# Norm factors as exp(-ln/2) on ScalarE in place of square root and reciprocal, with the last squares summed by TensorE and smaller last stores

## What is computed

```python
def rmsnorm(x, g):
    xf = x * lax.rsqrt(jnp.mean(x * x, axis=-1, keepdims=True) + 1e-6)
    return xf * g
def swiglu_ffn(x, g, w_in, w_out):
    h = rmsnorm(x, g) @ w_in
    gate, up = jnp.split(h, 2, axis=-1)
    return (jax.nn.silu(gate) * up) @ w_out
# the layer
x = x + 0.5 * swiglu_ffn(x, norm_ffn1, w_ffn1_in, w_ffn1_out)
parts = rmsnorm(x, norm_mix) @ w_in            # ssd head group and attention head group
y = concatenate([rmsnorm(ssd(parts), g1), rmsnorm(nsa(parts), g2)])
x = x + y @ w_out
x = x + mem_attend(rmsnorm(x, norm_mem_q), mem_kv(rmsnorm(mem, norm_mem_kv)))
x = x + 0.5 * swiglu_ffn(x, norm_ffn2, w_ffn2_in, w_ffn2_out)
y = rmsnorm(x, norm_final)
```

## Time and profile before

| | us |
|---|---|
| median of 3 runs | 2840.41 (2838.55 to 2842.89) |
| the profiled execution, whole time | 2840.38 |
| its span in the trace | 2838.7 |
| TensorE busy | 2697.9 (95%) |
| VectorE busy | 1418.0 (50%) |
| ScalarE busy | 717.4 (25%) |
| GpSimd busy | 344.1 (12%) |
| mean granted TensorE clock | 0.973 of full speed |

### The profile page before, as it was taken

How to read it: one execution, slowest core, us unless ns; L and a number is a source line. 1 busy time by engine, 2 the same in 40 slices (tenths; PEclk the granted TensorE clock), 3 DMA queues, 4 the chain that set the end, 5 groups by cost and what they waited for, 6 DMA issues and landing times. The chain is left out here.

```text
span 2838.7 us, 43914 instructions
## 1 busy us (share of the span) xinstructions
PE 2697.9 (95%) x17720; PEld 2529.8 (89%) x17720; DVE 1418.0 (50%) x2949; ACT 717.4 (25%) x1466; POOL 344.1 (12%) x294
## 2 busy tenths in 40 slices
PE   8999999999989998989789988899999999999996
PEld 7999999999989997879557765797899999999996
DVE  7444444444466222335567753676644444444445
ACT  5111111111042212212456652435411111111102
POOL 0000000000020000101157761220100000000003
PEclk9999999999999999989889998899999999999998
DMA  6111111111025325114120004102211111111101
GB/s 215 45 45 45 46 45 45 45 45 45 16 96 67 53 76 192 59 38 116 42 61 16 2 22 177 60 23 90 75 45 45 45 45 45 45 45 45 41 5 63
DMA packets 62989, 168.42 MB, mean 59 GB/s; under 512 B 10468, under 2 KB 43780, under 8 KB 52996
## 3 DMA queue, kind: packets, MB, share of 16 engines
q1 hardware_dynamic: 57716, 150.36, 16.8%
q10 hardware_dynamic: 3104, 9.41, 0.9%
q0 software_dynamic: 1968, 5.77, 0.6%
HBM read 145.90 MB, written 23.69 MB: 60 GB/s over the span
## 5 line engine op out<-in xcount | busy, mean ns | idle before, releaser
L523 DVE TENSOR_TENSOR ffn_gated<-ffn_gate_up,ffn_inv_rms 128x728 f32<-128x728 f32 x132 | 120.6, 914 | 536.9 <-PE ffn_gate_up L206 536.7
L204 PE MATMUL ffn_gate_up<-h_ffn_hi,ffn_up_hi 128*128 128x364 f32 (+1 forms) x1056 | 349.1, 331 | 15.1 <-DVE h_ffn_lo L102 11.5
L204 PE MATMUL ffn_down<-ffn_act_hi,ffn_down_hi 128*128 128x364 f32 (+1 forms) x1056 | 349.9, 331 | 7.8 <-issue 6.2
L204 PE MATMUL ffn_gate_up<-h_hi,ffn_up_hi 128*128 128x364 f32 (+1 forms) x1056 | 347.5, 329 | 2.6 <-DVE ffn_gated L523 1.0
L205 PE MATMUL ffn_gate_up<-h_ffn_lo,ffn_up_hi 128*128 128x364 f32 (+1 forms) x1056 | 347.8, 329 | 0.0
L205 PE MATMUL ffn_down<-ffn_act_lo,ffn_down_hi 128*128 128x364 f32 (+1 forms) x1056 | 347.8, 329 | 0.0
L206 PE MATMUL ffn_gate_up<-h_ffn_hi,ffn_up_lo 128*128 128x364 f32 (+1 forms) x1056 | 347.7, 329 | 0.0
L206 PE MATMUL ffn_down<-ffn_act_hi,ffn_down_lo 128*128 128x364 f32 (+1 forms) x1056 | 347.3, 329 | 0.0
L205 PE MATMUL ffn_gate_up<-h_lo,ffn_up_hi 128*128 128x364 f32 (+1 forms) x1056 | 346.9, 329 | 0.0
L206 PE MATMUL ffn_gate_up<-h_hi,ffn_up_lo 128*128 128x364 f32 (+1 forms) x1056 | 346.9, 328 | 0.0
L557 DVE SCALAR_TENSOR_TENSOR x<-ffn_down,x 128x364 f32<-128x364 f32 (+1 forms) x480 | 248.0, 533 | 148.0 <-PE ffn_down L206 148.0
(11 more groups left out here) (469 smaller groups left out, 4739.5 us busy)
## 6 DMA issues: line engine op xcount, KB each, us to landing
ffn_up_raw<-in_w_ffn_in SPq DMA_DIRECT2D x42, 1024.0 KB, 4.8
ffn_down_raw<-in_w_ffn_out SPq DMA_DIRECT2D x22, 1024.0 KB, 4.8
mix_w_raw<-in_w_mix SPq DMA_DIRECT2D x20, 512.0 KB, 3.4
scratch_x<-x SPq DMA_DIRECT2D x1, 4352.0 KB, 12.8
out_proj<-mix_stage ACTq DMA_DIRECT2D x8, 544.0 KB, 2.7
x<-scratch_x SPq DMA_DIRECT2D x1, 4352.0 KB, 16.9
cmp_w<-in_cmp_w SPq DMA_DIRECT2D x2, 2048.0 KB, 14.6
ssd_pages<-in_cmp_pages SPq DMA_DIRECT2D x32, 128.0 KB, 2.0
```

What stands on the lines that cost most here:

```text
L204: pe.matmul(out, w_hi, x_hi, start=start, stop=False)
L523: dve.tensor_tensor(zu[:, b, :, 0:w], gu[:, b, :, 0:w], inv[:, groups(g)].rearrange("p (o c) -> p o c", o=1).to_broadcast([P, 2, w]), ALU. ...
```

## The change

1. root and invert become one function, factor, on ScalarE: Ln of the mean square plus eps, then Exp with scale -0.5, in place. The semaphore from the root to DVE becomes one from Ln to Exp on ACT itself, and DVE waits for the Exp. All 22 reciprocals of norms go (3 in each of the ffn, mix and final norms, 9 in the out stage, 1 for the memory keys). In the out stage factor's Exp carries the waits that invert had.
2. A Ln of one column is added at the start of each ffn close and at the end of the sample attention, so that the table is loaded there.
3. In the final norm, factors 0 and 1 come behind square 11 and 19 in place of 12 and 20. The last tile's squares are no longer added by POOL: TensorE adds them with a second matmul into the same bank.
4. The last group's stores are four of 2 tiles, in place of two of 4.

```diff
-    def root(self, act, g):
+    def factor(self, act, g):
+        at = self.inv[:, groups(g)]
         if self.late is not None and g:
             act.wait_ge(self.late_summed, g)
-        act.activation(self.inv[:, groups(g)], self.sums[:, g, 0:width_of(g)], ACT.Sqrt, bias=self.core.eps[:, 0:1]
-                       ).then_inc(self.rms_ready, 1)
-    def invert(self, dve, g):
-        dve.wait_ge(self.rms_ready, g + 1)
-        dve.reciprocal(self.inv[:, groups(g)], self.inv[:, groups(g)]).then_inc(self.inv_ready, 1)
+        act.activation(at, self.sums[:, g, 0:width_of(g)], ACT.Ln, bias=self.core.eps[:, 0:1]).then_inc(self.log_ready, 1)
+        act.wait_ge(self.log_ready, g + 1)
+        act.activation(at, at, ACT.Exp, scale=-0.5).then_inc(self.inv_ready, 1)
...
+        mm = pe.matmul(out, self.ones[:], self.acc[g][:, 0:width_of(g)], start=True, stop=stop and direct is None)
+        if direct is not None:
+            pe.wait_ge(self.sq_ready, direct + 1)
+            mm = pe.matmul(out, self.ones[:], self.sq[direct % len(self.sq)][:, 0:width_of(g)], start=False, stop=stop)
+        mm.then_inc(self.summed, 1)
...
         for g in range(GROUPS):
+            size = KT // 2 if g < GROUPS - 1 else 2
+            for k in range(0, KT, size):
+                sp.wait_ge(self.y_ready, g * KT + k + size)
...
                 def close():
+                    act.activation(log_table[:], core.eps[:, 0:1], ACT.Ln)
...
-                        if fin is not None and d in (KT + lag, 2 * KT + lag):
-                            fin.roots(act, d // KT - 1)
+                        if fin is not None and d in (KT + lag - 1, 2 * KT + lag - 1):
+                            fin.factor(act, d // KT - 1)
...
                     rounds(2)
-                    root(1)
-                    root(2)
+                    factor(1)
+                    factor(2)
                     split_up(1, 1, False)
...
                 def factor(g):
-                    parts.invert(dve, g)
                     dve.wait_ge(parts.inv_ready, g + 1)
+                    if g == 2:
+                        dve.wait_ge(act_ready, 1)
                     scale(0, 0, g)
...
-                def root(i):
+                def factor(i):
...
+                    act.activation(logs[:, i % 2, 0:c], ms[:, i % 2, 0:c], ACT.Ln, bias=core.eps[:, 0:1]
+                                   ).then_inc(log_ready, 1)
+                    act.wait_ge(log_ready, i + 1)
+                    if i >= 3:
+                        old = UNITS[i - 3]
+                        act.wait_ge(h_ready[old[0:2]], KT if old[0] == "x" else 4 * (old[2] + 1))
+                    act.activation(inv[:, i % 3, 0:c], logs[:, i % 2, 0:c], ACT.Exp, scale=-0.5).then_inc(inv_ready, 1)
```

More of the change, by code:

```diff
@@ L156, in add, with sum @@
         pool.tensor_tensor(acc, acc, sq, ALU.add).then_inc(self.added, 1)
-    def sum(self, pe, g, last, stop=True):
+    def sum(self, pe, g, last, stop=True, direct=None):
+        out = self.bank(g)[:, :width_of(g)]
         pe.wait_ge(self.added, last + 1)
-        pe.matmul(self.bank(g)[:, :width_of(g)], self.ones[:], self.acc[g][:, 0:width_of(g)], start=True, stop=stop
-                  ).then_inc(self.summed, 1)
-class FinalNorm:
[L168 to L174, removed]
-        act.wait_ge(self.running.summed, g + 1)
[L176 to L186, removed]
@@ L397, in _ @@
                     rounds(1)
-                    root(0)
+                    factor(0)
                     head_squares(1)
@@ L1574, in _ @@
                 rounds(1)
-                parts.root(act, 0)
+                parts.factor(act, 0)
                 rounds(2)
-                parts.root(act, 1)
-                parts.root(act, 2)
+                parts.factor(act, 1)
+                parts.factor(act, 2)
                 split(2)
@@ L2721, in _ @@
                 act.wait_ge(ms_ready, 1)
-                act.activation(inv[:], ms[:, 0:W], ACT.Sqrt, bias=core.eps[:, 0:1]).then_inc(rms_ready, 1)
+                act.activation(inv[:], ms[:, 0:W], ACT.Ln, bias=core.eps[:, 0:1]).then_inc(log_ready, 1)
+                act.wait_ge(log_ready, 1)
+                act.activation(inv[:], inv[:], ACT.Exp, scale=-0.5).then_inc(inv_ready, 1)
                 for n in range(2 * MT):
@@ L2978, in _ @@
                     for n in range(KT):
-                        for i in roots_at(g, n):
-                            root(i)
+                        for i in factors_at(g, n):
+                            factor(i)
                         if g == 0 and n + 2 < KT:
@@ L2990, in _ @@
                 query_hi(0, 0)
-                root(index["x", 2])
+                factor(index["x", 2])
                 round_hi("x", 2, 0)
```

83 lines of the change are left out of this document (39 added, 44 removed).

## The result

The changed kernel takes 2849.69 us, median of 20 runs (2838.13 to 2860.22); the kernel before took 2840.43 in 20 runs beside them (2836.33 to 2856.14). The ratio is 1.0030, with a 95% interval from 1.0017 to 1.0042: **8.5 us slower**, between 4.8 and 11.9. The forecast was 2847.6, range 2842.0 to 2852.5.

The account below looks back on a forecast made before the run. TensorE, busy 95% of the span, was taken to bound the kernel, with VectorE alone ending the last close. 0.35 + 6.8 + 5.0 - 4.95 = +7.2 on 2840.38 gave 2847.6 us, range 2842.0 to 2852.5.

Parts of the forecast that it names:

- second ffn head: wait, clock: Head of the second ffn stage: TensorE stands still 4.9 us before product 3, the clock's fall costs 1.9; together +6.8.
- out stage: Out stage: later factors delay weight and normed lo parts, TensorE waits and the clock falls once; +5.0 us.
- first ffn head: Head of the first ffn stage: factor 1 comes later, product 3 starts some 0.8 later; +0.35 us, bounds 0 and 0.8.
- mix, memory keys, tables: Mix stage, memory keys and other stages' table loads: no net cost, 0 us, bounds -1.3 and +0.3.
- last close, VectorE: Last close: factors come sooner, the direct sum saves nothing, VectorE ends 4.05 us sooner.
- stores: Last close: stores of 2 tiles carry half the bytes and land sooner; -0.9 us.
- The loads: Every factor: Ln and Exp stand in different table sets, so loads are real, each costing 1.30 us on ScalarE.
- first rival: Whole kernel: one table set serves Ln and Exp, loads cost next to nothing; about 2824 us, chance 5%.
- P5's wait: Out stage, group 0: w_lo(5) comes late, so TensorE waits 0.8 to 1.0 us at product P5.
- P7 and the squares behind it: Out stage, group 0: the delay runs on to product P7, 0.5 us more, and to group 0's squares, 0.5 more.
- P16's extra: Out stage, group 1: lo parts for product P16 come late, 2.0 to 2.8 us more TensorE idle; 2.0 taken.
- One fall of the clock: Out stage: waits at product P16 and for POOL behind it let the clock fall once, 1.5 us; it may stay out.

Follow-up runs that it names:

- head_order: Changed kernel with the weights of split_up(1, 1) rounded and subtracted earlier at the second ffn head; 2845.62 us, 1.0009 of before.
- out_before: Changed kernel with the out stage's nine factors as square root and reciprocal again; 2846.09 us, 1.0014 of before.
- fixed_two: Changed kernel with split_up(1, 1) rounded ahead of factors 1 and 2 at the second ffn head and the out stage as before; 2836.98 us, 0.9983.
- close_only: Kernel before with only the change's final norm and last close; 2837.36 us, 0.9976 of before.
- close_half_stores: Kernel before with only the last close's change, but the last group stored in two parts of 4 tiles; 2836.43 us, 0.9982.
- no_exp: Changed kernel with a Copy of the same scale in place of Exp in all 22 factors; 2821.23 us, 0.9924 of before.
- close_split: Kernel before with only the last close's change, factor 1 behind square 18, and TensorE taking square 22 directly too; 2836.69 us, 0.9973.

## Why the prediction was right

| term | forecast | measured | by |
|---|---|---|---|
| second ffn head: wait, clock | +4.9, +1.9 | +4.98, 2.2 to 2.8; stage +7.2 | trace; head_order -7.8, out_before +7.2 |
| out stage | +5.0 | +5.3 to +5.7 | out_before |
| first ffn head | +0.35 | product 3 +1.0; first close 0 to 2.4 later | four traces |
| mix, memory keys, tables | 0 | within 1 us at equal clock | fixed_two |
| last close, VectorE | -4.05 | -4.1 (5.3 less 1.2 of clock) | close_only, head_order |
| stores | -0.9 | -1.0 | close_half_stores |
| sum | +7.2 | +8.5 (4.8 to 11.9) | 20 runs |

**The loads.** The forecast hung on them, and no_exp shows it did so rightly: without them the changed kernel is faster than before by 21.6 us, close to the first rival's 2824. One step of the reasoning was wider than its row: the earlier trace rows show that the set in use behind that Exp did not hold Ln, not that no set holds both. It was the list of the built program that settled it.

**The second head** went as reckoned, to 0.1 us in the wait. The clock's part was between the two bounds given.

**The out stage.** The mechanism was right, w_lo(5) and then the lo parts for P16, but that the sum came out is in part luck. P5's wait was put at 0.8 to 1.0 and is 1.14; P7 and the squares behind it were put at 1.0 and cost 0.9 against the trace of before, but only 0.3 against that of close_only, whose stage is the same. P16's extra was put at 2.0 and is 0.9. One fall of the clock was counted, 1.5 us, and two came, at 1848 and at 1887, 9 and 6 matmuls, which cost 1.6 and 1.5. The comparison behind the one fall was wrong as well: at their lower end 1.7 and 1.30 are 3.0 us of idle, not more than 2.60 + 0.66. The start was put at -0.4; P2 starts 1.8 sooner than before, but of that some 1.8 is the low stretch at the stage's start, 21 matmuls before and 8 now (an estimate, 13 times 0.14). From the stage's start to P24 the changed kernel loses 4.6 us against before. The last 1.0 of the stretch's 5.6 arises in the memory attention, where the clock falls behind a wait of 2.2 us in eleven of the twelve traces, kernels with the stage as before among them, and did not in the one of before: no effect of the change.

**The first head is the undersized term.** "Product 3 starts some 0.8 later" held: it waits 2.52 where it waited 1.74, and starts 1.0 later. I let product 4's 0.3 of idle absorb part of that, and that idle is gone. What failed is "+0.35; bounds 0 and 0.8": I had read in the rows that 1.74 costs no clock and that 2.60 does, and did not apply it to this wait of 2.5. Of four traces of kernels with this head, the clock fell behind product 3 in two (the changed kernel, from 42.91, and out_before, at 41.91) and not in two (head_order, fixed_two). Where it fell, 9 to 11 matmuls took 0.14 more, 1.3 to 1.5 us, and the first close started 2.4 and 1.2 later than before; where it did not, 0.0 and 0.8. In the changed kernel:

```profile
42.00 0.40 PE L204 MATMUL ffn_gate_up<-h_ffn_hi,ffn_up_hi 128*128 128x364 f32 x1 [2.52 <-DVE ffn_gated L529]
...
42.73 0.38 PE L205 MATMUL ffn_gate_up<-h_ffn_lo,ffn_up_hi 128*128 128x364 f32 x1
42.91 0.51 PE L206 MATMUL ffn_gate_up<-h_ffn_hi,ffn_up_lo 128*128 128x364 f32 x1
```

**The close.** The steps held one by one: factor 0 earlier, factor 1 bound by ScalarE's four steps, the direct sum worth nothing, y 16 at 38.7 us behind the close's first matmul by the forecast and 37.44 + 1.2 = 38.6 measured at the same clock. What I did not see is that VectorE's two new waits, 1.8 and 2.8, were left for the taking, and that the second is GpSimd's.

**What the sum leaves.** Second head, out, first head and close add up to 7.4 at least and 10.2 at most by the traces, and 8.5 was measured, between 4.8 and 11.9: the medians can't tell the forecast of 7.2 from any of these. Whether the ssd and nsa stages, which took 3.1 us more in the changed kernel's trace, lose anything from the change is not shown; with all kernels between 658.0 and 668.4, the longest in close_split, which holds the change only in its close, and no order by whether they hold the change, I take it as chance. The chances were added up loosely: 0.8 x 51 + 14 + 2 is 57, not 58.

## What to carry to other kernels

Before you replace a function of one table set by two functions, list the loads that the build puts in: here a chain of Ln and Exp cost two loads of 1.28 us nearly each time, whatever one set could hold, and it gains only where nobody waits behind them. When an engine that is mostly idle gets more work, look at what stands behind it in its queue, and move the item that the bound engine needs to the front: one item moved forward in two queues gave back 7.8 us of its stage here, with every load still in place. And a matmul that replaces an add saves nothing when it runs behind the other adds; a matmul laid in the wait saved a whole add, 1.20 us.

## What the hardware showed that I had not expected

- **A table load does not wait for the next activation's semaphore.** In the changed kernel the load at 2838.66 runs in ScalarE's idle time, and the Ln follows at 2842.51 when PE's sum comes. This load costs nothing; those of the second head, which stand between activations of one chain, cost 1.30 each.
- **The clock falls behind waits of about 2.5 us in some executions and not in others**: at the first head after 2.52 once yes and once no, after 2.53 no, after 2.60 yes; after a wait of 2.2 in the memory attention in eleven traces of twelve. At the two ffn heads it never fell after 1.00 and 1.74, and each time after 3.03 and 4.98. Two shorter waits close together can be enough: behind 0.70 and 1.30 (P8) it fell in the changed kernel, at 1848, and not in out_before, which has the same two. The low stretch at the last close, always behind the same 3.10 of idle, was 9 to 13 matmuls in eight traces and 19 or 20 in four, 1.2 us apart.
- **The same instructions took 658.0 to 668.4 us** in the stages between, with the granted clock. A difference of two single profiled executions (13.5 here) can be half again the difference of the medians (8.5 to 9.3); only a stage's own duration, from a point behind the last disturbance, is good to 0.1.
